# A scan and a delta-rule pass on one core: where the second begins, and where its helper work stands

## The chip, the core and the metric

The kernel runs on one core of a Trainium2 chip. TensorE (PE) multiplies, VectorE (DVE), ScalarE (ACT) and GpSimd (POOL) do elementwise work, and SyncE (SP) issues most DMAs. Each engine takes its instructions strictly in its own program order and waits on semaphores that others raise. The metric is the device time of one execution in microseconds (us), the median of three runs. All times below are in us.

## The reference

The reference is two transformer-like blocks over 1024 tokens of width 1024. The change lies in the first block's mixer, which has three branches that are concatenated:

- windowed attention with sinks (4 heads),
- a state-space scan (8 heads), with a state carried from chunk to chunk,
- a gated delta rule (4 heads of 64). For each chunk it solves a unit lower triangular system and then runs a recurrence over the chunks:

```
strict = tril((kbeta k^T) * decay, -1)
u, w   = solve(I + strict, [v*beta, kbeta*exp(g)])
v_new  = u - w state
o      = (q*exp(g)) state + (q k^T * decay) v_new
state  = state*exp(g_last) + (k*exp(g_last-g))^T v_new
```

The mixed output goes through `w_out`, and then a feed-forward and a second block of attention and gated mixing follow.

## The kernel before, in words

Tokens are cut into 8 chunks of 128. All engines walk one list, `schedule(units)`, of items `(kind, argument)`. Each engine's program is that list, filtered to the kinds that it has work for, so an item's place in the list sets its place in the queue of every engine that it touches. PE's products for such items go through four PSUM banks in rotation: a product needs its bank's earlier content read, four products before.

**The scan** (one iteration per chunk c, line 186 on) treats attention and state space together: `sa` makes the decay exponentials of a chunk (PE, then ACT L1256), `sg` multiplies them by C·B (DVE L1665), `as` scores and row maxima (PE L885, DVE L1618 to L1623, ACT exponentials L1231), `ap` transposes the attention weights (PE L893, copied by ACT L1237 and DVE L1629), `ao` applies them (PE L906, DVE L1635), `yo` and `yd` are the two parts of the output (DVE L1726, L1731), `st` updates the state `Sst` (PE L988, DVE L1734) and has POOL gate the output (L751 to L755). POOL also scales the inputs of a chunk (`xc`, L746, L748) as part of `sa`; its second scaling waits for ACT.

**The inverses.** The delta rule's triangular systems are inverted by blocks. The 32x32 diagonal blocks of all chunks and heads lie on the 128 partitions of one tile `AB` (they came there through DRAM), and DVE inverts them all together in 31 elimination steps, items `inv`, each a multiply (L1675) and a subtract (L1677) over up to 16x16 elements. Six steps stand at the end of each scan chunk from chunk 1 on, so the 31st, with a copy (L1679), stands in chunk 6. SP then stores both results to DRAM and loads them back as blocks with 16 DMAs into `qkv` (L688 to L695, semaphore `x_in`). In SP's program this stands behind the loads of `z` for the scan (L642), of which the one for chunk 7 waits until chunk 5 is gated.

**The delta pass** handles chunk c with these items: `gx` expands the 32-blocks into the block-diagonal 128x128 matrices `X` and `XT` (8 ACT instructions of L1287; POOL scales keys and values into `kbv`, L763 to L765), `ly` and `lx` (PE L958 and L970, read out by DVE L1695, L1702, L1704) merge blocks to size 64 (level 5) and 128 (level 6), `uw` applies the inverse (PE L994, L997, copied by ACT L1298), `r1` and `r2` are the recurrence (PE L1004 to L1012, DVE L1709 to L1717, ACT squares L1274). X, XT and Y have three buffers. The order is software-pipelined: iteration c runs the recurrence of chunk c, level 6 of chunk c+1, level 5 of chunk c+2, and at its end the expansion of chunk c+3.

**The norms.** `sn` 0 and `sn` 1 normalise the scan's output for chunks 0 to 3 and 4 to 7: a reciprocal square root in 12 short DVE instructions (L1412 to L1418), then 8 ACT instructions (L1270). `gn` is the like for the delta rule (DVE, then POOL). `mx` transposes everything for the product with `w_out`.

Of the kernel before, what the change touches and what calls it, by code (L numbers as in the profile page):

```python
# [25 lines left out]
NT = T // P  # L26
# [114 lines left out]
NORMED = (3, 6, 7)  # L141
# [7 lines left out]
def schedule(units):  # L149

    by = {u["kind"]: n for n, u in enumerate(units)}
    s, late, begun = [], [], set()

    def begin(kds, before, between):

        begun.update(kds)
        s.extend(before + [("half", (by[kd], 0)) for kd in kds] + between + [("half", (by[kd], 1)) for kd in kds])
# [26 lines left out]
    steps = iter(range(31))  # L184
    s += [("sa", 0), ("as", 0), ("sg", 0), ("sa", 1), ("yo", 0)]
    for c in range(NT):
        more = c + 1 < NT
        s += [("yd", c), ("ap", c), ("st", c)] + [("sg", c + 1), ("as", c + 1)] * more + [("ao", c)]
        s += [("yo", c + 1)] * more + [("sa", c + 2)] * (c + 2 < NT) + [("inv", n) for n in islice(steps, 6 * (c > 0))]
        s += [("sn", c // 4)] * (c % 4 == 3)  # L190
    assert next(steps, None) is None


    def at(kind, c, lv=None):
        return [(kind, c if lv is None else (c, lv))] if 0 <= c < NT else []
# [1652 lines left out]
```

How the kernel before makes its waits and increments, by code:

```python
        def gemm_product(eng, n):  # L494
            eng.wait_ge(gemm_done[n % 2], wide(n) // 2 + 1)
# [1 line left out]
        def gemm_consumed(eng, n):  # L498
            eng.wait_ge(gemm_read[n % 2], wide(n) // 2 + 1)
# [1 line left out]
        def scores_product(eng, h):  # L502
            w = scores_number(h)
            eng.wait_ge(gemm_done[w % 2], w // 2 + 1)
            return G[w % 2]
# [1 line left out]
        def scores_consumed(eng, h):  # L508
            w = scores_number(h)
            eng.wait_ge(gemm_read[w % 2], w // 2 + 1)
# [1 line left out]
        def side_product(eng, key):  # L513
            p = prod[key]
            eng.wait_ge(side_done[p % 4], p // 4 + 1)
            return S[p % 4]
# [1 line left out]
        def side_consumed(eng, key):  # L519
            p = prod[key]
            eng.wait_ge(side_read[p % 4], p // 4 + 1)
# [7 lines left out]
            def __call__(self, ins, name=None):  # L530
                s = N[name] if name else self.own
                self.count[name] = self.count.get(name, 0) + 1
                ins.then_inc(s, 1)
                self.eng.wait_ge(s, self.count[name])
# [1 line left out]
            def frees(self, ins, key):  # L536
                p = prod[key]
                ins.then_inc(side_read[p % 4], 1)
                self.eng.wait_ge(side_read[p % 4], p // 4 + 1)
# [1 line left out]
            def frees_gemm(self, ins, n):  # L542
                ins.then_inc(gemm_read[n % 2], 1)
                self.eng.wait_ge(gemm_read[n % 2], wide(n) // 2 + 1)
# [89 lines left out]
            def load_z(c):  # L635
                if c >= 2:
                    sp.wait_ge(N["gated"], c - 1)
                else:
```

## Time and profile before

| | us |
|---|---|
| runs | 2437.78, 2437.77, 2436.27 |
| median | 2437.77 |
| the profiled execution, its own time | 2435.77 |
| its span, first to last instruction | 2433.9 |
| mean granted TensorE clock, share of full | 0.965 |
| PE busy | 2224.6 (91%) |
| DVE, ACT, POOL busy | 954.6, 697.1, 621.2 |
| the scan, first to last chunk | 386 to 512 |
| the delta pass, first to last product | 523.8 to 615.5 |

A "busy" time adds up what an engine's instructions took; the chain of waits says which of them set the end. Positions are us from the start of the span. The granted clock is a share of 2.4 GHz; 0.50 is 1.2 GHz. "Idle before" in a timeline row is how long an engine stood in front of that instruction, and the name behind the arrow is whose end released it.

### The profile page before, as it was taken

To read this page: it belongs to the slowest core of one execution; us is meant where nothing else is said; L and a number is where in the kernel's file an instruction comes from. 1 tells how busy PE (TensorE), PEld (TensorE's weight loads), DVE (VectorE), ACT (ScalarE), POOL (GpSimd) and SP (SyncE) were. 2 spreads that over 40 slices of the span, in tenths; PEclk is the share of its full clock that TensorE was granted. 3 is DMA by queue.
4 is the path that set the end of the run, shared out by engine and by line. 5 is a ranking of instruction groups with operands and counts; after the bars stand their busy time and mean duration, and the time that the engine had idled before them with its cause. 6 is when DMAs were issued, how large, how long until landed. Compare 5 with 4: busy or idle time off the path is not lost.

```text
span 2433.9 us, 28528 instructions
## 1 busy us (share of the span) xinstructions
PE 2224.6 (91%) x11363; PEld 1878.0 (77%) x11363; DVE 954.6 (39%) x1429; ACT 697.1 (29%) x1478; POOL 621.2 (26%) x399
## 2 busy tenths in 40 slices
PE   6999988768987999999999996978999999999896
PEld 5888877667777888888888875767888888888775
DVE  4445316856315101211121125678995235111123
ACT  4332135444333111000000005327775122000134
POOL 2233322322221323323233331220000233233321
PEclk9999999779998999999999997999999999999998
DMA  4111310020310111111111110300001111111121
GB/s 147 44 44 44 93 33 24 18 70 1 104 44 27 45 51 52 44 53 44 52 52 44 52 44 27 114 27 10 1 1 31 44 45 43 52 48 48 52 95 69
DMA packets 179475, 117.51 MB, mean 48 GB/s; under 512 B 25252, under 2 KB 171408, under 8 KB 179216
## 3 DMA queue, kind: packets, MB, share of 16 engines
q1 hardware_dynamic: 165984, 91.77, 13.0%
q10 hardware_dynamic: 13360, 23.92, 2.8%
q8 instruction: 90, 1.47, 0.3%
q14 instruction: 41, 0.34, 0.0%
HBM read 102.57 MB, written 13.11 MB: 48 GB/s over the span
## 4 chain that ended last, share of the span: by engine, by line
PE 73%; DVE 18%; ACT 5%; issue 2%; SPq 1%; DMA 0%; ACTq 0%; DVEq 0%
PE gemm L811 21%; PE gemm L813 21%; PE gemm L812 21%; DVE PT L1426 3%; DVE a2m L1787 3%; PE side L842 2%; PE side L822 2%; PE side L970 1%; DVE x L1749 1%; ACT sqp L1112 1%; DVE rpd L1591 1%; PE side L1047 1%; DVE w_raw L1677 1%; PE side L958 1%; ACT Eg L1246 0%
## 5 line engine op out<-in xcount | busy, mean ns | idle before, releaser
L811 PE MATMUL gemm<-h_hi,w_hi 128*128 128x512 f32 x1968 | 773.8, 393 | 8.2 <-DVE h_lo L1819 8.2
L813 PE MATMUL gemm<-h_hi,w_lo 128*128 128x512 f32 x1968 | 768.3, 390 | 0.0
L812 PE MATMUL gemm<-h_lo,w_hi 128*128 128x512 f32 x1968 | 768.0, 390 | 0.0
L714 POOL TENSOR_SCALAR w_hi<-w_raw 128x1024 fp32r<-128x1024 f32 x153 | 170.3, 1113 | 1539.5 <-PE gemm L813 1524.3
L811 PEld LDWEIGHTS gemm<-h_hi,w_hi 128*128 128x128 f32 x1968 | 370.6, 188 | 86.1 <-issue 8.1
L813 PEld LDWEIGHTS gemm<-h_hi,w_lo 128*128 128x128 f32 x1968 | 370.3, 188 | 77.5
L812 PEld LDWEIGHTS gemm<-h_lo,w_hi 128*128 128x128 f32 x1968 | 370.8, 188 | 75.0
L716 POOL TENSOR_TENSOR w_lo<-w_raw,w_hi 128x1024 fp32r<-128x1024 f32 x153 | 374.4, 2447 | 12.8
L1450 DVE TENSOR_TENSOR ft<-sg,gemm 128x1024 f32<-128x1024 f32 x22 | 26.9, 1221 | 382.1 <-PE gemm L813 382.1
L811 PE MATMUL gemm<-f_hi,w_hi 128*128 128x512 f32 x352 | 138.9, 395 | 4.9 <-DVE f_lo L1452 4.9
L1160 ACT ACTIVATE f_hi<-ft 128x1024 fp32r<-128x1024 f32 x22 | 23.4, 1064 | 414.2 <-DVE ft L1450 414.2
L813 PE MATMUL gemm<-f_hi,w_lo 128*128 128x512 f32 x352 | 138.1, 392 | 0.0
L812 PE MATMUL gemm<-f_lo,w_hi 128*128 128x512 f32 x352 | 138.1, 392 | 0.0
L1456 DVE TENSOR_TENSOR accT<-accT,gemm 128x1024 f32<-128x1024 f32 x40 | 48.8, 1221 | 172.3 <-PE gemm L813 172.1
L1445 DVE SCALAR_TENSOR_TENSOR cacc<-cin,cols,cacc 128x1024 f32<-128x1024 f32 x42 | 67.4, 1606 | 89.3 <-ACT cacc L1132 88.3
L1059 PE MATMUL side<-PT,vp 128*128 128x256 f32 x512 | 92.4, 302 | 0.4 <-DVE PT L1426 0.4
L1426 DVE TENSOR_TENSOR PT<-side,PT 128x512 fp32r<-128x512 f32 x128 | 88.5, 691 | 10.0 <-ACT PT L1369 6.2
L1369 ACT ACTIVATE PT<-side 128x512 fp32r<-128x512 f32 x128 | 76.5, 598 | 44.2 <-PE side L1047 39.9
L1047 PE MATMUL side<-con,Pb 128*128 128x128 f32 x512 | 77.9, 276 | 9.5 <-DVE aoT L1803 9.5
L811 PEld LDWEIGHTS gemm<-f_hi,w_hi 128*128 128x128 f32 x352 | 66.8, 190 | 18.9 <-issue 5.3
L1470 DVE TENSOR_TENSOR yT<-sig,gemm 128x1024 f32<-128x1024 f32 x8 | 9.8, 1221 | 181.8 <-PE gemm L813 181.8
L1787 DVE TENSOR_REDUCE a2m<-gemm 128x1 f32<-128x1024 f32 x64 | 78.4, 1224 | 5.8 <-PE gemm L1038 3.6
(348 smaller groups left out, 2719.5 us busy)
## 6 DMA issues: line engine op xcount, KB each, us to landing
w_raw<-in_w_in SPq DMA_DIRECT2D x60, 512.0 KB, 3.8
w_raw<-in_ffn_w_gate SPq DMA_DIRECT2D x22, 512.0 KB, 3.8
w_raw<-in_ffn_w_up SPq DMA_DIRECT2D x22, 512.0 KB, 3.8
w_raw<-in_ffn_w_down SPq DMA_DIRECT2D x22, 512.0 KB, 3.5
w_raw<-in_w_out SPq DMA_DIRECT2D x16, 512.0 KB, 4.2
xin<-in_x SPq DMA_DIRECT2D x8, 512.0 KB, 6.7
x<-in_x ACTq DMA_DIRECT2D x1, 4096.0 KB, 15.4
x_spill<-x ACTq DMA_DIRECT2D x2, 2048.0 KB, 7.1
```

The source lines that it names most:

```text
L714: gp.tensor_scalar(whi[w % 2][:], raw[w % 4][:], 1.0, 0.0, ALU.mult, ALU.add).then_inc(pool_hi, 1)
L716: gp.tensor_tensor(wlo[w % 2][:], raw[w % 4][:], whi[w % 2][:], ALU.subtract).then_inc(w_split, 1)
L811: mm(o, hi[:, k, m], act[0][:, k, t], start=k == 0, stop=False)
L812: mm(o, hi[:, k, m], act[1][:, k, t], start=False, stop=False)
L813: last = mm(o, lo[:, k, m], act[0][:, k, t], start=False, stop=k == kt - 1)
L1047: last = tr(b[:, hslice(i)], Pb[(2 * m + i % 2) % 4][:, hslice(2 * q + i // 2)], ident)
L1059: last = mm(b[:, 0:256], vp[:, 2 * q + i, m % 4 // 2, :], PT[q][part][:, 256 * i:256 * i + 256], start=q == 0 and i == 0 and part == 0, st ...
L1369: step(af(PT[q][0][:], b[:], ACT.Copy), "hi_ready")
L1426: ins = v.tensor_tensor(dst, b, hi, ALU.subtract)
L1445: step(v.scalar_tensor_tensor(out=buf[:], in0=cin[:, i:i + T], scalar=cols[:, wcol:wcol + 1], in1=buf[:], op0=ALU.mult, op1=ALU.add), "con ...
L1456: step.frees_gemm(v.tensor_tensor(accT[:, j[1], :], accT[:, j[1], :], g[:], ALU.add), n)
L1787: step(v.reduce_max(mx, g[:], axis=AX))
```

## The change

Only the list in `schedule` changes. The elimination steps stand eight to a chunk from chunk 1 on, so that the last stands in chunk 4. The last scan chunk also takes in the first items of the delta pass (`gi`, three `gx`, the merges of chunk 0, level 5 of chunk 1, `uw` of chunk 0). In the delta pass `gx` stands at the start of an iteration instead of the end, and `sn` 1, which stood at the end of the scan, stands at the end of the pass's iteration 1. Line numbers of the changed kernel are 2 higher from there on.

```diff
@@ -185,20 +185,22 @@
     s += [("sa", 0), ("as", 0), ("sg", 0), ("sa", 1), ("yo", 0)]
     for c in range(NT):
         more = c + 1 < NT
-        s += [("yd", c), ("ap", c), ("st", c)] + [("sg", c + 1), ("as", c + 1)] * more + [("ao", c)]
-        s += [("yo", c + 1)] * more + [("sa", c + 2)] * (c + 2 < NT) + [("inv", n) for n in islice(steps, 6 * (c > 0))]
-        s += [("sn", c // 4)] * (c % 4 == 3)
+        if more:
+            s += [("yd", c), ("ap", c), ("st", c), ("sg", c + 1), ("as", c + 1), ("ao", c), ("yo", c + 1)]
+            s += [("sa", c + 2)] * (c + 2 < NT) + [("inv", n) for n in islice(steps, 8 * (c > 0))] + [("sn", 0)] * (c == 3)
+        else:
+            s += [("gi", 0), ("gx", 0), ("yd", c), ("ap", c), ("ly", (0, 5)), ("gx", 1), ("st", c), ("lx", (0, 5)), ("ao", c)]
+            s += [("ly", (0, 6)), ("ly", (1, 5)), ("lx", (0, 6)), ("lx", (1, 5)), ("uw", 0), ("gx", 2)]
     assert next(steps, None) is None
 
 
     def at(kind, c, lv=None):
         return [(kind, c if lv is None else (c, lv))] if 0 <= c < NT else []
 
-    s.append(("gi", 0))
-    for c in range(-3, NT):
-        s += at("ly", c + 1, 6) + at("r1", c) + at("ly", c + 2, 5) + at("lx", c + 1, 6) + at("r2", c)
-        s += at("lx", c + 2, 5) + at("uw", c + 1) + at("gx", c + 3)
-        s += [("gn", n) for n in range(len(NORMED) - 1) if NORMED[n] == c]
+    for c in range(NT):
+        s += at("gx", c + 3) + at("ly", c + 1, 6) + at("r1", c) + at("ly", c + 2, 5) + at("lx", c + 1, 6) + at("r2", c)
+        s += at("lx", c + 2, 5) + at("uw", c + 1)
+        s += [("gn", n) for n in range(len(NORMED) - 1) if NORMED[n] == c] + [("sn", 1)] * (c == 1)
     begin([("wo", 0), ("wo", 1)], [("mx", 0)], [("gn", len(NORMED) - 1), ("mx", 1), ("load", 0)])
     run([("wo", j) for j in range(8)], lambda kd: [(0, ("woT", kd[1]))])
     flush()
```

No instruction is added or taken away on any engine; the places move. Names are buffers, `x4` is four like instructions in a row.

**ACT, end of the scan, before.** From the row sums of the last scan chunk's scores (`asb`) to the second read-out of a solved block (`uw`); `X_148`, `X_149`, `X_150` are the three expansion buffers.
```order
L1231 ACTIVATE asb,asum<-asb,anm 128x256 x4
L1232 ACTIVATE ads<-ads 128x4
L1237 ACTIVATE apT<-side 128x512
L1264 ACTIVATE mixs_145,nss_s<-xs 128x256 x2
L1270 ACTIVATE xs<-xs,nrs_s 128x256 x8
L1287 ACTIVATE X_148<-qkv,con 128x4x32 x4
L1287 ACTIVATE XT_151<-qkv,con 128x4x32 x4
L1287 ACTIVATE X_149<-qkv,con 128x4x32 x4
L1287 ACTIVATE XT_152<-qkv,con 128x4x32 x4
L1298 ACTIVATE uw_157<-side 128x512
L1287 ACTIVATE X_150<-qkv,con 128x4x32 x4
L1287 ACTIVATE XT_153<-qkv,con 128x4x32 x4
```

The same stretch of ACT in the changed kernel:
```order
L1233 ACTIVATE asb,asum<-asb,anm 128x256 x4
L1234 ACTIVATE ads<-ads 128x4
L1289 ACTIVATE X_148<-qkv,con 128x4x32 x4
L1289 ACTIVATE XT_151<-qkv,con 128x4x32 x4
L1239 ACTIVATE apT<-side 128x512
L1289 ACTIVATE X_149<-qkv,con 128x4x32 x4
L1289 ACTIVATE XT_152<-qkv,con 128x4x32 x4
L1266 ACTIVATE mixs_145,nss_s<-xs 128x256 x2
L1300 ACTIVATE uw_157<-side 128x512
L1289 ACTIVATE X_150<-qkv,con 128x4x32 x4
L1289 ACTIVATE XT_153<-qkv,con 128x4x32 x4
L1289 ACTIVATE X_148<-qkv,con 128x4x32 x4
```

The expansions of chunks 0 and 1 moved ahead of the copy of `apT` and of the squares, and the eight instructions of L1270 left this stretch.

**ACT inside the delta pass, before.** From the squares of chunk 0's output (`gsq`) on; `uw_158` and `uw_157` are the copies that chunk 1's and chunk 2's recurrence need.
```order
L1274 ACTIVATE gsq,nss_g<-qkv 128x64 x4
L1298 ACTIVATE uw_158<-side 128x512
L1287 ACTIVATE X_148<-qkv,con 128x4x32 x4
L1287 ACTIVATE XT_151<-qkv,con 128x4x32 x4
L1274 ACTIVATE gsq,nss_g<-qkv 128x64 x4
L1298 ACTIVATE uw_157<-side 128x512
L1287 ACTIVATE X_149<-qkv,con 128x4x32 x4
L1287 ACTIVATE XT_152<-qkv,con 128x4x32 x4
L1274 ACTIVATE gsq,nss_g<-qkv 128x64 x4
```

The same stretch in the changed kernel:
```order
L1276 ACTIVATE gsq,nss_g<-qkv 128x64 x4
L1300 ACTIVATE uw_158<-side 128x512
L1289 ACTIVATE X_149<-qkv,con 128x4x32 x4
L1289 ACTIVATE XT_152<-qkv,con 128x4x32 x4
L1276 ACTIVATE gsq,nss_g<-qkv 128x64 x4
L1300 ACTIVATE uw_157<-side 128x512
L1272 ACTIVATE xs<-xs,nrs_s 128x256 x8
L1289 ACTIVATE X_150<-qkv,con 128x4x32 x4
L1289 ACTIVATE XT_153<-qkv,con 128x4x32 x4
L1276 ACTIVATE gsq,nss_g<-qkv 128x64 x4
L1300 ACTIVATE uw_158<-side 128x512
```

The expansion (`X`, `XT`) moved from behind the `uw` copy to ahead of the squares, and the eight instructions on `xs` now stand between the copy of `uw_157` for chunk 2 and the expansion behind it.

**PE, last scan chunk, before.** `E_139` is that chunk's decay matrix, `asb` the attention weights, `Bt` and `av` the state update and the attention output; `SQ_114` belongs to chunk 0 of the delta rule.
```order
L985 MATMUL side<-xc_141,E_139 128x64 x8
L893 MATMUL side<-con,asb 128x128 x8
L988 MATMUL side<-xc_141,Bt 128x256 x2
L906 MATMUL side<-av,apT 128x64 x8
L958 MATMUL side<-X_148,SQ_114 128x128 x4
L970 MATMUL side<-Y_154,XT_151 128x128 x4
L970 MATMUL side<-XT_151,Y_154 128x128 x4
L958 MATMUL side<-X_148,SQ_114 128x128 x4
L958 MATMUL side<-X_149,SQ_115 128x128 x4
```

The same stretch in the changed kernel:
```order
L987 MATMUL side<-xc_141,E_139 128x64 x8
L895 MATMUL side<-con,asb 128x128 x8
L960 MATMUL side<-X_148,SQ_114 128x128 x4
L990 MATMUL side<-xc_141,Bt 128x256 x2
L972 MATMUL side<-Y_154,XT_151 128x128 x4
L972 MATMUL side<-XT_151,Y_154 128x128 x4
L908 MATMUL side<-av,apT 128x64 x8
L960 MATMUL side<-X_148,SQ_114 128x128 x4
L960 MATMUL side<-X_149,SQ_115 128x128 x4
```

The first merge product (`X_148`, `SQ_114`) moved ahead of the state update, and two more ahead of the attention output.

## Rows read from the trace of the kernel before

**Rows 1.** Windows by stage: length, busy PE, PEld, DVE, ACT, POOL, clock, DMA, GB/s.
```profile
414.65:429.10 14.45, 12.22 (x77) 10.89 (x77) 13.08 (x32) 7.73 (x25) 6.88 (x6) 0.88 0.07 19
443.47:462.25 18.78, 11.48 (x69) 9.11 (x68) 17.38 (x41) 10.18 (x30) 7.05 (x7) 0.74 0.06 16
462.25:484.32 22.07, 17.52 (x85) 15.23 (x86) 14.97 (x29) 9.34 (x28) 5.70 (x6) 0.73 0.04 12
484.32:497.58 13.26, 12.02 (x79) 10.86 (x79) 12.27 (x29) 7.72 (x25) 3.48 (x5) 0.91 0.07 21
512.20:523.83 11.63, 0.00 (x1) 0.00 (x1) 2.64 (x14) 7.29 (x17) 0.62 (x1) 0.50 0.86 190
523.83:537.69 13.86, 12.17 (x81) 11.20 (x81) 5.37 (x8) 3.19 (x8) 0.00 (x0) 0.74 0.22 54
537.69:604.30 66.61, 53.16 (x459) 50.58 (x457) 39.86 (x79) 31.21 (x102) 16.38 (x26) 0.97 0.01 1
```
**Rows 2.** Windows of DVE alone, in which it has no wait: length, busy, clock, DMA, GB/s.
```profile
420.83:425.80 4.97, 4.17 (x15) 0.94 0.01 3
435.22:436.75 1.53, 1.40 (x4) 1.00 0.00 0
436.75:440.17 3.42, 3.15 (x8) 1.00 0.00 0
449.57:458.95 9.38, 8.54 (x24) 0.66 0.00 1
449.60:453.26 3.66, 3.39 (x9) 0.90 0.00 0
474.45:481.02 6.57, 6.13 (x12) 1.00 0.00 0
490.41:494.28 3.87, 3.42 (x14) 1.00 0.00 0
503.71:505.25 1.54, 1.44 (x4) 0.50 0.00 0
512.20:514.91 2.71, 2.30 (x12) 0.50 0.78 123
```
**Rows 3.** Timeline of DVE, then POOL, chunk 3: start, us, operation.
```profile
450.96 0.42 DVE L1677 TENSOR_TENSOR w_raw<-w_raw,w_raw 128x252 f32<-128x252 f32 x1
...
454.63 1.14 DVE L1677 TENSOR_TENSOR w_raw<-w_raw,w_raw 128x252 f32<-128x252 f32 x1
...
454.29 1.21 POOL L748 TENSOR_TENSOR xc<-xc,ed 128x512 f32<-128x512 f32 x1 [8.30 <-ACT ed L1258]
```
**Rows 4.** Timeline of SP's queue: the last spill load of the scan.
```profile
484.50 0.32 SPq L642 DMA_DIRECT2D zs<-z_spill  x1
```
**Rows 5.** Chain of waits, before the first expansion.
```profile
517.55 2.72 DMA qkv<-x_blocks
```
**Rows 6.** Timeline of ACT: end of scan, start of pass; idle before in brackets.
```profile
504.20 0.20 ACT L1232 ACTIVATE ads<-ads 128x4 f32<-128x4 f32 x1
...
514.97 4.29 ACT L1270 ACTIVATE xs<-xs,nrs_s 128x256 f32<-128x256 f32 x8 [5.14 <-DVE nrs_s L1418]
520.34 1.70 ACT L1287 ACTIVATE X<-qkv,con 128x128 f32<-128x128 f32 x4 [1.08 <-DMA qkv<-x_blocks]
...
537.87 0.60 ACT L1298 ACTIVATE uw<-side 128x512 f32<-128x512 f32 x1 [10.62 <-PE side L997]
538.49 1.70 ACT L1287 ACTIVATE X<-qkv,con 128x128 f32<-128x128 f32 x4
...
546.00 0.26 ACT L1274 ACTIVATE gsq<-qkv 128x64 f32<-128x64 f32 x1 [4.07 <-DVE qkv L1714]
```
**Rows 7.** Timeline of PE: state update and attention output of the last scan chunk.
```profile
506.22 1.92 PE L988 MATMUL side<-xc,Bt 128*128 128x256 f32 x4
507.92 3.52 PE L906 MATMUL side<-av,apT 128*128 128x64 f32 x16
```
**Rows 8.** Waits in 537.69 to 604.30: us in total, times, longest.
```profile
PE side L958 <- ACT XT L1287: 13.5, 6, 2.2
```

## The prediction, made before the changed kernel was run

> **What bounds the kernel now.** I read the page's chain of waits first. It lies on PE for 73% of the span, nearly all of it in the large products, which the change leaves alone. The 240 us that it touches lie at 386 to 622, where the chain passes between engines, so I cut that stretch into windows [rows 1].
>
> A scan chunk takes 13.26 us when little else is in it, and in the one window of that length DVE still holds six inverse steps. The next window to look at is 512.20 to 523.83: 11.63 us in which PE does nothing. The last scan product has ended and the first merge product waits for an expansion, which waits for the inverses to come back from DRAM: the last of 16 loads lands at 517.55 + 2.72 = 520.27 [rows 5], ACT expands from 520.34 [rows 6], and DVE had the inverses ready at 505.25 [rows 2]. So the return trip is 15.0 us. Then come 13.86 us of lead-in, partly at half clock, before iteration 0 of the pass [rows 1].
>
> In the pass PE stands in front of its level 5 product six times, 13.5 us in all, always for ACT's expansion [rows 8], which ACT can only start behind its `uw` copy [rows 6]. In that window PE is busy 53.2 of 66.6 us, DVE 39.9, ACT 31.2 [rows 1].
>
> **What the change costs in the scan.** Call the inverse stretch the time on DVE between the end of its update of `Sst` (L1727) and the start of `mixs` (L1731). In chunk 1 it is 4.97 us and the chunk 14.45; in chunk 5 it is 3.87 and the chunk 13.26 [rows 1, 2]. What exceeds about 3.8 us lengthens the chunk one for one; below that, ACT's exponentials are last anyway. Chunk 3 fits: 9.38 - 3.85 + 13.26 = 18.79, measured 18.78.
>
> With eight steps a chunk, the stretches become:
> - Chunk 1: 4.97 + steps 7 and 8, 1.53 = 6.50.
> - Chunk 2: steps 9 to 12, 3.42, and 13 to 16, 3.66 = 7.1.
> - Chunk 3: its present 9.38 loses steps 13 to 16 (3.66) and gains steps 19 to 24, which take 6.57 in chunk 4, of which 1.4 is the stall below = 10.9.
> - Chunk 4: steps 25 to 30, 3.87, and step 31 with the copy, 1.54 = 5.4.
> - Chunks 5 and 6: none, and that gains nothing, since they were hidden there.
>
> Now the stall. A DVE step of 252 elements takes 0.42 us, but 1.14 when it begins after POOL's `xc` has begun [rows 3], and two such losses of 0.72 are in the 9.38 of chunk 3 and in the 6.57 of chunk 4. POOL's two instructions begin 4.72 us after the stretch does (449.57 to 454.29). The stretches of chunks 1 and 2 end at about that point now, and will reach past it. I add 1.4 to each of the first two and to chunk 4: 7.9, 8.5, 10.9, 6.8, against 4.97, 5.0, 9.38, 6.57. The scan grows by 3.0 + 3.5 + 1.5 + 0.2 = 8.2 us. Without any new stall it would be 5.3 (chunks 3 and 4 keep theirs), and if all are dodged 2.5.
>
> The Trainium skill says under "SBUF — State Buffer", section "SBUF: two separate sides", that DVE and POOL share a port pair as an exclusive lock: a DVE operation with two inputs in SBUF and a POOL operation that reads SBUF exclude each other for a whole instruction. By that rule every step that meets `xc` waits it out, and the rule speaks against longer stretches. The 1.14 against 0.42 above agrees, and a sum that ignored the rule would come out 2.9 us lower.
>
> PE also idles longer while DVE works, and after such idle time it comes back at 1.2 GHz: chunk 3's window has a clock of 0.74, and in chunk 4, 22.07 us long, 16.0 would follow from its 6.57 us stretch. Of the other 6.0, 4.3 is `sn` 0 on ACT (eight instructions like those at 514.97 [rows 6]), which leaves 1.7 for the clock. I take 1.5 us more in total, bounds 0 and 12 (twice those 6.0). Scan: +9.7.
>
> **What is gained between scan and pass.** Times here are those of before; the scan's delay is already counted. The inverses are ready at the end of chunk 4. SP must first issue the spill load that waits for chunk 5's gating (484.50 [rows 4]), so the return trip runs from there to about 484.8 + 15.0 = 499.8. ACT wants it at 504.40, when the last attention row is done [rows 6]. The margin is 4.6 us, and a longer scan shifts both alike. SP has nothing else queued between the two.
>
> The two halves of an expansion, X and XT, take 1.7 us each, 3.5 with the gap [rows 6], so PE's first merge product starts at 508.0 instead of 523.83: 15.8 earlier. From there to iteration 0 took 13.86. Into that now fall the state update, 1.92, and the attention output, 3.52 [rows 7], at half clock. The first lies where PE waited for DVE's read-out of Y (PE was idle 1.7 of the 13.86 [rows 1]), the second does not. PE has no long idle time before it, so some of this stretch may run at 2.4 GHz; I take the addition as 3.1 us, 1.92 + 3.52 less 1.7 and less 0.6 for this. Gain 12.7. The bounds: all at full clock 13.7; all at half clock, as the first half of the lead-in did, about 5.5.
>
> Queued behind the inserted work: ACT's copy of `apT` waits 3.5 us for the expansion, and `ao` waits for that copy. ao is then read at about 518, and only `zg` and weight loads on SP wait for it, needed 100 us later. POOL makes `kbv` of chunks 0 and 1 ahead of the gating, about 4 us, which nobody needs before `mx`. `uw` of chunk 0 is copied before the third expansion, as it was, so iteration 0 keeps its wait of 2.24.
>
> **What is gained in the pass.** From iteration 1 on the expansion stands one iteration ahead, so five of six waits go: 5 x 2.24 = 11.2. What is late next is PE itself: 66.6 / 6 = 11.1 us per iteration less 2.24 is 8.9, and PE is busy 53.2 / 6 = 8.9; ACT needs 31.2 / 6 = 5.2 and DVE 6.6 [rows 1].
>
> Two things lose their cover. `sn` 1 ran at 512 to 519, while everyone waited for the loads. Now its 2.71 us on DVE [rows 2] and 4.29 on ACT [rows 6] stand at the end of iteration 1. Behind them on ACT come the expansion 3.5, the squares about 1.5 and the `uw` copy 0.6: 12.6 us from the last `uw` copy to the end of the next, where PE wants the recurrence about 8.8 after it. Cost 3.8 us. And `gn` 0, 12 like instructions on DVE after iteration 3, was hidden by PE's 2.24 wait; without it about 0.9 of its 2.5 shows. Bounds: 2.0 for both if ACT's idle time absorbs more, 7.0 (2.71 + 4.29) if nothing overlaps. Pass: 11.2 - 3.8 - 0.9 = 6.5.
>
> **The sum.** 12.7 + 6.5 - 9.7 = 9.5 us less. The profiled execution took 2435.77 (span 2433.9 and 1.9 around it), which is 2.0 below the median of 2437.77. From the one, 2426.3; from the other, 2428.3. I predict 2428 for the median. Everything behind 622 shifts as a block: weights arrive and are split on their own queues, well ahead.
>
> **Rivals.**
> 1. *No stall, and a warm lead-in.* DVE's longer stretch slips between POOL's instructions, or the clock returns early. For: chunk 2's present stretch just misses `xc`. Against: POOL starts 4.72 after the stretch begins, whatever DVE does. 12.7 + 6.5 - 5.3 = 13.9, and 2424; with the lead-in at its best 2423.
> 2. *The pass does not speed up.* The expansion is early, but another wait takes its place, for instance the banks or the read-outs on DVE, busy 40 us of the 67. Against: DVE has over 2 us of room in each iteration of 8.9. The pass then gains nothing and still pays 4.7: 12.7 - 4.7 - 9.7 = -1.7, that is 2439, no change.
> 3. *PE's clock, the slower side.* The place is chunks 2 to 4 and the lead-in. If PE's idle gap behind each longer DVE stretch brings 1.2 GHz for most of the next chunk, as in the 22.07 us chunk, scores and decay products come late, DVE waits for them, and the gap grows again. Price: 6.0 in each of two more chunks, and the lead-in at its worst, 5.5. 5.5 + 6.5 - 8.2 - 12 = -8.2: 2446. It decides from about 12 us of extra scan time over the 8.2 with a cold lead-in; half of it gives no change. For it: 0.74 and 0.73 in rows 1. Against: chunk 1 ran at 0.88 and fits the formula without any clock term.
> 4. *The inverses come late.* If the return trip takes over 4.6 us longer beside the scan, ACT stands at the expansion with `apT` behind it, and each us more costs one. With 20 us in place of 15: hardly 1; with 25: 2434.
>
> The Trainium skill, "TensorE: Matmul & The Clock Gate", section "HAM oscillation — how this bites in real kernels", describes rival 3 as a rule: waits inside a loop re-throttle PE, and each round starts cold. Followed to the letter it gives the time of rival 3. The clock of 1.00 in the DVE windows of chunks 2 and 4 [rows 2] disagrees so far, the 0.66 of chunk 3 agrees.
>
> **Chances.** The forecast 58%, rival 1 18%, rival 2 8%, rival 3 8%, rival 4 8%. What the kernel's measurement can tell from no change is about 0.2%, 4.9 us, so faster ends at 2432.9. Forecast and rival 1 are on that side but for a few in a hundred, as is half of rival 4: 78%. Rival 2, the rest of rival 4, half of rival 3: 16%. Slower 6%. The range, 2419 to 2436, holds the first two with their bounds and most of rival 4.
>
> **What would show it.** In the new profile: PE's idle time in front of the first merge product about 1.5 us; the SP loads done before ACT's last attention exponential; waits of PE L960 on ACT's XT once, not six times; iterations of 8.6 to 8.9 us but for those behind iterations 1 and 3; DVE steps of 1.1 us in chunks 1 and 2; chunk lengths near 17.4, 17.9, 20.3 and 22 to 24. The forecast is wrong if the loads end behind 504 + 9.7, if chunks 5 and 6 got shorter than 13.26, or if the pass's six iterations take over 63 us (66.6 - 6.5 = 60.1 expected).

## The result, and the profile after

| | us |
|---|---|
| changed kernel, 4 runs | 2419.55 median (2418.59 to 2419.96) |
| kernel before, 4 runs beside it | 2437.78 median (2436.27 to 2442.52) |
| ratio | 0.9921, 95% interval 0.9904 to 0.9939 |
| profiled execution after: own time, span, mean clock | 2419.96, 2418.1, 0.969 |

The kernel got 18.2 us faster (0.8%), where 9.8 was forecast (2428 against 2419.55): the sign was right, and the forecast was about half of what came. From span to span the two profiled executions differ by 15.8 us (2433.9 to 2418.1). The rest of the 18.2 is that the profiled execution of before was 2.0 us quicker than its median and that of the changed kernel 0.4 slower.

First the same windows as in [rows 1], in the profile of the changed kernel: chunks 1 to 5, from the last chunk's scores to the first merge product, the lead-in, iterations 0 to 5, and the rest up to the first product with `w_out`. Columns as there.

```profile
413.77:431.22 17.45, 12.01 (x77) 10.48 (x77) 15.94 (x36) 7.73 (x25) 8.04 (x7) 0.86 0.05 16
431.22:449.99 18.77, 13.52 (x79) 11.62 (x79) 16.90 (x34) 7.72 (x25) 5.72 (x6) 0.86 0.05 14
449.99:470.20 20.21, 12.20 (x75) 10.07 (x74) 18.67 (x45) 10.18 (x30) 5.71 (x6) 0.75 0.05 15
470.20:492.66 22.46, 17.60 (x85) 15.17 (x86) 15.26 (x33) 9.34 (x28) 5.73 (x6) 0.73 0.04 12
492.66:505.82 13.16, 11.93 (x79) 10.78 (x78) 8.84 (x17) 7.73 (x25) 3.38 (x5) 0.92 0.60 152
505.82:516.16 10.34, 6.10 (x47) 5.54 (x46) 7.80 (x17) 6.86 (x22) 5.10 (x7) 0.95 0.23 36
516.16:530.62 14.46, 14.46 (x100) 13.71 (x100) 6.64 (x11) 4.81 (x13) 4.60 (x5) 0.80 0.32 93
530.62:589.77 59.15, 52.59 (x458) 50.43 (x456) 41.87 (x91) 35.31 (x110) 16.42 (x26) 0.97 0.06 15
589.77:607.45 17.68, 12.78 (x107) 11.23 (x105) 12.89 (x32) 7.98 (x25) 4.02 (x6) 1.00 0.00 1
```

Set against before, stretch by stretch:

| stretch | before | after | less by |
|---|---|---|---|
| start of chunk 1 (untouched code) | 414.65 | 413.77 | 0.9 |
| chunks 1 to 5 | 14.45, 14.37, 18.78, 22.07, 13.26 | 17.45, 18.77, 20.21, 22.46, 13.16 | -9.1 |
| chunk 6's start to iteration 0 | 40.11 | 24.80 | 15.3 |
| iterations 0 to 5 | 66.61 | 59.15 | 7.5 |
| iteration 6 to `w_out` | 17.68 | 17.68 | 0.0 |
| from there on (untouched code) | 1811.92 | 1810.65 | 1.3 |

**The scan.** These are the windows of DVE's inverse stretches of chunks 1 to 4, which answer to [rows 2].

```profile
419.93:427.92 7.99, 7.03 (x19) 0.91 0.01 2
438.04:446.69 8.65, 8.07 (x18) 1.00 0.00 0
456.08:466.91 10.83, 9.84 (x29) 0.71 0.00 0
482.39:489.36 6.97, 6.42 (x16) 1.00 0.00 0
```

Forecast were 7.9, 8.5, 10.9 and 6.8. The stall that was to come into chunk 1 is there. In DVE's and then POOL's timeline of that chunk, two steps of over 1 us, each beside one POOL instruction, stand in front of one of 0.36, as in [rows 3]:

```profile
424.92 1.06 DVE L1677 TENSOR_TENSOR w_raw<-AB,w_raw 128x175 f32<-128x175 f32 x1
426.02 1.08 DVE L1679 TENSOR_TENSOR w_raw<-w_raw,w_raw 128x175 f32<-128x175 f32 x1
427.14 0.36 DVE L1677 TENSOR_TENSOR w_raw<-AB,w_raw 128x192 f32<-128x192 f32 x1
...
424.66 1.12 POOL L750 TENSOR_TENSOR xc<-xc,ed 128x512 f32<-128x512 f32 x1 [7.25 <-ACT ed L1260]
425.87 1.04 POOL L753 TENSOR_TENSOR xs<-xs,dskip 128x512 f32<-128x512 f32 x1
```

**The return trip and the start.** SP's timeline, then ACT's, at the end of the scan:

```profile
492.84 0.32 SPq L644 DMA_DIRECT2D zs<-z_spill  x1
498.98 8.63 SPq L697 DMA_DIRECT2D qkv<-x_blocks  x16
...
512.44 0.20 ACT L1234 ACTIVATE ads<-ads 128x4 f32<-128x4 f32 x1
512.67 1.71 ACT L1289 ACTIVATE X<-qkv,con 128x128 f32<-128x128 f32 x4
```

The trip to DRAM begins right behind the spill load that waits for chunk 5 (492.84), the last of the 16 loads is issued by 498.98 + 8.63 = 507.6, and ACT goes from its last attention row (512.44) into the expansion without a gap [rows 4 to 6 for before]. PE's idle time in front of the first merge product is 2.38 us instead of 12.39 (about 1.5 was forecast). Its timeline from there:

```profile
516.16 2.07 PE L960 MATMUL side<-X,SQ 128*128 128x128 f32 x8 [2.38 <-ACT XT L1289]
518.03 1.91 PE L990 MATMUL side<-xc,Bt 128*128 128x256 f32 x4
519.74 1.91 PE L972 MATMUL side<-Y,XT 128*128 128x128 f32 x8
521.44 1.34 PE L972 MATMUL side<-XT,Y 128*128 128x128 f32 x8
522.62 1.90 PE L908 MATMUL side<-av,apT 128*128 128x64 f32 x16
```

The attention output took 1.90 here and not the 3.52 of [rows 7]: the clock came back to 2.4 GHz in the second merge (the granted clock is 0.50 up to 522.0, which is 5.9 us behind the start of the first merge product, and 0.97 from there to 522.62). In before it was 0.50 up to 531.0, 7.2 us behind that product. From the first merge product to iteration 0 it is 14.46 us, where 13.86 + 3.1 = 17.0 were forecast.

**The pass.** PE's waits in iterations 0 to 5, against the six of [rows 8]:

```profile
PE side L1006 <- issue: 2.5, 1, 2.5
PE side L960 <- ACT XT L1289: 2.2, 1, 2.2
PE side L972 <- DVE Y L1697: 1.8, 2, 0.9
```

The iterations take 12.46, 8.32, 9.44, 11.09, 9.52 and 8.32 us (before 10.83, 10.83, 12.45, 10.83, 10.84, 10.83). The 12.46 and the 12.45 are the same thing: 1.6 us of half clock behind a wait, which falls into one iteration of each kernel. The "issue" wait of 2.5 us stands in front of the recurrence of the 11.09 us iteration, and ACT's timeline shows what is late there:

```profile
551.58 0.60 ACT L1300 ACTIVATE uw<-side 128x512 f32<-128x512 f32 x1 [1.21 <-PE side L999]
554.52 4.29 ACT L1272 ACTIVATE xs<-xs,nrs_s 128x256 f32<-128x256 f32 x8 [2.34 <-DVE nrs_s L1420]
...
563.84 0.60 ACT L1300 ACTIVATE uw<-side 128x512 f32<-128x512 f32 x1
```

12.3 us from one `uw` copy to the next, because `sn` 1 stands between them (12.6 had been worked out).

### The profile page after: what moved, and what is told of

Read it like the earlier page. It is cut to its first block, busy times and chain, and to the rows that moved or that the text cites. A ratio compares the mean times of both kernels' runs of the same rounds, so it can differ in the third digit from the quotient of the medians.

```text
span 2418.1 us, 28528 instructions
## 1 busy us (share of the span) xinstructions
PE 2218.9 (92%) x11363; PEld 1873.2 (77%) x11363; DVE 957.3 (40%) x1429; ACT 697.7 (29%) x1478; POOL 621.7 (26%) x399
## 4 chain that ended last, share of the span: by engine, by line
PE 74%; DVE 18%; ACT 5%; issue 2%; SPq 0%; DMA 0%; ACTq 0%; DVEq 0%
PE gemm L813 21%; PE gemm L815 21%; PE gemm L814 21%; DVE PT L1428 3%; DVE a2m L1789 3%; PE side L844 2%; PE side L824 2%; DVE x L1751 1%; PE side L972 1%; ACT sqp L1114 1%; DVE rpd L1593 1%; DVE w_raw L1677 1%; DVE w_raw L1679 1%; PE side L1049 1%; PE side L960 1%
## 5 line engine op out<-in xcount | busy, mean ns | idle before, releaser
L1452 DVE TENSOR_TENSOR ft<-sg,gemm 128x1024 f32<-128x1024 f32 x22 | 26.9, 1221 | 382.0 <-PE gemm L815 382.0
L1428 DVE TENSOR_TENSOR PT<-side,PT 128x512 fp32r<-128x512 f32 x128 | 88.5, 691 | 10.1 <-ACT PT L1371 6.2
```

The costliest lines, as they stand in the source:

```text
L1428: ins = v.tensor_tensor(dst, b, hi, ALU.subtract)
```

## The experiments

Each ratio is to runs of the kernel before that were taken beside it: its median was 2436.95 for the first four kernels below, 2438.47 for the next four, 2436.73 for e8 to e10, and 2439.61 for e11. Where a text compares with the changed kernel, its 2419.6 is meant.

### The changed kernel once more (a0)

No edit; a yardstick for what repeats.

> The changed kernel once more, as the yardstick of this group. Its profiled span was 15.8 us below before's, its median 18.2. Theory (the profiled windows hold the whole effect): 14.5 us between 386 and the first w_out product, so a median 14 to 17 below before, and 18.2 was partly scatter. Rival (a real gain outside that stretch): 18 or more again.

2419.72 (2418.69 to 2420.82), ratio 0.9926 [0.9912, 0.9940]. Span 2418.9, chunks 17.45, 18.77, 20.24, 22.50, 13.17, iterations 12.46, 8.32, 9.45, 11.09, 9.52, 8.32, and 1810.7 from `w_out` on. The median is 17.2 below that of before, which is just above the theory's 14 to 17 and below the rival's 18. In these two profiled executions even the patches of half clock fall in the same places. That this holds for every execution of a program isn't shown: the kernel before was profiled once, and its executions range from 2433.5 to 2443.7, at mean clocks from 0.963 to 0.968.

### Eight steps alone (e1)

```diff
 kernel before:
-... [("inv", n) for n in islice(steps, 6 * (c > 0))]
+... [("inv", n) for n in islice(steps, 8 * (c > 0))]
```

> Before with eight elimination steps per chunk and nothing else. Theory: the scan grows by 9.1 us as in the changed kernel (chunks 1 to 4 about 17.5, 18.8, 20.2, 22.5), the inverses are back before the scan ends, but ACT still has sn 1 in front of the first expansion, so the first merge product stands at 519.3 + 0.3 + 3.5 + 9.1 = 532 instead of 523.8: slower than before by 8. Rival (the return trip from DRAM was the bound, so having it early pays by itself): the 11.6 us gap shrinks to under 3 and the kernel is faster than before.

2443.68 (2442.60 to 2447.79), ratio 1.0028 [1.0017, 1.0038]: 6.7 us slower than before, where 8 was expected. Chunks 17.45, 18.78, 20.22, 22.44, 13.17, those of the changed kernel to 0.03 us. The first merge product stands at 528.52 (before 523.83), since the end of the scan and `sn` 1 behind it (on ACT until 525.00), not the return trip, now decide. From the start of chunk 1 to iteration 0 it is 5.8 us more than before. Iterations 0 to 4 are as before, but iteration 5 took 12.46 instead of 10.83 and the stretch from iteration 6 to `w_out` 18.7 instead of 17.7, in code without an edit. So the steps' own cost is 5.8 us by the trace. It is real, and by itself it buys nothing.

### Expansion one iteration ahead alone (e2)

```diff
 kernel before:
-        s += at("ly", c + 1, 6) + at("r1", c) + at("ly", c + 2, 5) + ...
+        s += at("gx", c + 3) * (c >= 0) + at("ly", c + 1, 6) + at("r1", c) + at("ly", c + 2, 5) + ...
...
-        s += at("lx", c + 2, 5) + at("uw", c + 1) + at("gx", c + 3)
+        s += at("lx", c + 2, 5) + at("uw", c + 1) + at("gx", c + 3) * (c < 0)
```

> Before with gx of the pass at the start of an iteration and nothing else. Theory: five of six waits on ACT's XT go, each worth 2.5 us (10.83 to 8.32 per iteration), gn 0 shows 1.2 us: 12.5 - 1.2 = 11.3 faster. My prediction priced a wait at 2.24: 11.2 - 0.9 = 10.3. Rival (the early start of the pass is what pays): under 5.

2422.42 (2416.47 to 2425.33), ratio 0.9937 [0.9923, 0.9951]: 14.5 us faster than before, the greatest part of the change, where 11.3 was expected; its six runs scatter by 9 us. Iterations 10.83, 8.33, 8.32, 8.32, 9.53, 8.32 = 53.65, 13.0 less than 66.61. That is 5 x 2.51 = 12.5 for the waits, 1.6 for the clock patch that is gone, and 1.2 lost where `gn` 0 now shows (9.53). `sn` 1 still stood in the gap of the return trip and cost nothing.

### The early start with six steps a chunk (e4)

```diff
 changed kernel:
-... [("inv", n) for n in islice(steps, 8 * (c > 0))]
+... [("inv", n) for n in islice(steps, 6 * (c > 0))]
```

> The changed kernel with six elimination steps per chunk, so that the last stands in chunk 6. Theory: the scan is 9.1 us shorter, but the inverses are ready only at 505 and land at 520.3 (positions of before), ACT stands at the first expansion with the copy of apT behind it, the merge product starts at 523.8, and with state update and attention output behind it iteration 0 starts 14.5 later at 538.3, against 531.5 in the changed kernel: 7 us slower than the changed kernel, 8 to 9 faster than before. Rival (the scan's growth costs more than the early return is worth): faster than the changed kernel.

2428.69 (2425.31 to 2428.90), ratio 0.9961 [0.9948, 0.9974]: 9.0 slower than the changed kernel, where 7 was expected. The chunks are those of before, but the first merge starts at 523.55. So eight steps, which lose 6.7 alone, gain 9.0 here (by the trace from chunk 1 to iteration 0: 5.8 lost, 5.6 gained): only both together bring the start forward. And this kernel is 6.3 slower than e2, which has none of the early start. Its iterations 0 to 5 take 60.7 us, 7.0 more than in e2: 3.9 is `sn` 1, which has lost its cover and gets nothing for it, and 3.1 are patches of half clock (iterations of 12.35 and 12.72).

### The second norm behind the pass (e3)

```diff
 changed kernel:
-        s += [... if NORMED[n] == c] + [("sn", 1)] * (c == 1)
-    begin(..., [("mx", 0)], [("gn", len(NORMED) - 1), ("mx", 1), ("load", 0)])
+        s += [... if NORMED[n] == c]
+    begin(..., [("mx", 0)], [("sn", 1), ("gn", len(NORMED) - 1), ("mx", 1), ("load", 0)])
```

> The changed kernel with sn 1 moved out of the pass to behind the first half of mx, where ACT is idle for 10 us and DVE for 7. Theory: the 1.1 us that PE waits for DVE's read-out of Y in iteration 2 and the 2.8 us before the recurrence of chunk 3 both go: 3.9 us faster than the changed kernel, iterations 2 and 3 of the pass 8.32 each. Rival (sn 1 is hidden there by slack): no change. Second rival: it now delays the second half of mx, and up to 2 us come back there.

2419.06 (2418.18 to 2421.42), ratio 0.9923 [0.9911, 0.9935]: 0.7 faster by the times, too little to tell from nothing. In the trace the pass is what was expected, iterations 12.47, 8.32, 8.32, 8.32, 9.53, 8.33 = 55.29, 3.9 less than 59.15, and the second half of `mx` comes no later. So `sn` 1 did cost 3.9. Chunks 3 to 5 were 2.1 us shorter, too. But the stretch from iteration 6 to `w_out` took 19.0 here instead of 17.7, at a clock of 0.82 where it was 1.00, and what is behind `w_out` 1812.9 instead of 1810.7; with that most of the gain is gone again. The 19.0 isn't the new place of `sn` 1, for e2 has 19.0 as well, without that edit. The last section shows one of the places behind `w_out`.

### POOL's multiply behind its wait (e5)

```diff
 changed kernel, POOL, item st:
-   step(gp.tensor_tensor(h64(xs[:, c, :]), h64(xs[:, c, :]), widen(dskip[:], 64), ALU.mult))
    side_consumed(pool, (("yd", c), 0))
+   step(gp.tensor_tensor(h64(xs[:, c, :]), h64(xs[:, c, :]), widen(dskip[:], 64), ALU.mult))
```

> The changed kernel with POOL's multiplication by dskip behind its wait for yd instead of ahead of it, so that only one POOL instruction instead of two falls into each inverse stretch of DVE. Theory (DVE steps wait for a POOL instruction that has begun): one DVE instruction of 1.1 us less per chunk, stretches of chunks 1 to 4 shorter by 0.7 each, 2.9 us faster than the changed kernel. Rival (the slow DVE steps are something else, for instance the steps' own shapes): no change, and the slow steps stay in number.

2416.65 (2415.33 to 2417.38), ratio 0.9911 [0.9898, 0.9923]: 3.1 faster than the changed kernel, where 2.9 was expected. The same steps of chunk 1 (DVE, then POOL) show one long step instead of two:

```profile
425.64 1.06 DVE L1677 TENSOR_TENSOR w_raw<-AB,w_raw 128x175 f32<-128x175 f32 x1
426.73 0.34 DVE L1679 TENSOR_TENSOR w_raw<-w_raw,w_raw 128x175 f32<-128x175 f32 x1
...
425.38 1.13 POOL L750 TENSOR_TENSOR xc<-xc,ed 128x512 f32<-128x512 f32 x1 [7.25 <-ACT ed L1260]
428.73 1.04 POOL L754 TENSOR_TENSOR xs<-xs,dskip 128x512 f32<-128x512 f32 x1 [2.23 <-DVE mixs L1733]
```

Chunks 1 and 2 are 0.73 us shorter each (16.72, 18.04), the price of one collision. DVE's stretches of chunks 3 and 4 are shorter, too (10.1 and 5.4 instead of 10.8 and 7.0; in chunk 4 two collisions went). Chunk 3 stayed at 20.25 all the same, because its stretch began 0.7 later in the chunk. Chunks 4 and 5 are 19.00 + 14.14 instead of 22.46 + 13.16: 2.5 less, of which 1.5 is the shorter stretch and the rest goes with the clock (0.85 instead of 0.73 in chunk 4). That the total fits the expected 2.9 is luck: the lead-in and iteration 0 were another 2.9 shorter by the clock, and the code behind the pass took 3.5 longer.

### State update and attention output ahead of the pass's items (e6)

```diff
 changed kernel:
-            s += [("gi", 0), ("gx", 0), ("yd", c), ("ap", c), ("ly", (0, 5)), ("gx", 1), ("st", c), ("lx", (0, 5)), ("ao", c)]
+            s += [("gi", 0), ("yd", c), ("ap", c), ("st", c), ("ao", c), ("gx", 0), ("ly", (0, 5)), ("gx", 1), ("lx", (0, 5))]
```

> The changed kernel with the last scan chunk's own items (yd, ap, st, ao) ahead of the first expansion and merge. Theory (the interleaving fills PE's waits of the lead-in): ACT's expansion starts after the copy of apT at about 514.4, ends at 518, PE runs st and ao in its shadow; the first merge product stands 2 us later than 516.2, the lead-in is about 2.5 us shorter: within 1 us of the changed kernel. My prediction's pricing (2.4 to 3.8 us for st and ao in the lead-in) would make it 1 to 2 us faster. Rival (keeping PE busy early brings 2.4 GHz back early, which this order loses): 3 us or more slower.

2426.89 (2425.05 to 2428.32), ratio 0.9953 [0.9941, 0.9965]: 7.3 slower, where the theory had under 1 and the rival 3 or more. The first merge product comes 14.65 us behind the start of the last window of the scan (DVE's second product with `E`) instead of 10.34. ACT, which takes its items in order, copied `apT` at 515.05, then stood at the squares until POOL had gated (517.51), and began the expansion only at 518.59. The lead-in took 15.62 instead of 14.46, with 16 products of L960 at half clock (3.79 instead of 2.00). Together that is 5.5 us. The rest isn't the edit's: in the profiled execution chunk 1 began 3.8 later than in the changed kernel, in code that is the same.

### Both norms late (e7)

```diff
 e3, and in it:
-            s += [...] + [("inv", n) ...] + [("sn", 0)] * (c == 3)
+            s += [...] + [("inv", n) ...]
...
-        s += [... if NORMED[n] == c]
+        s += [... if NORMED[n] == c] + [("sn", 0)] * (c == 4)
```

> As e3 (sn 1 behind the first half of mx), and sn 0 also out of the scan, to the end of iteration 4 of the pass. Theory: chunk 3's stretch loses 2.4 us of DVE, chunk 4 loses 4.3 us of ACT and part of its slow clock (22.5 to about 17 to 18); in the pass it costs about 1.2 on DVE and under 1 on ACT. Sum: 2.4 + 4.3 + 1 - 2 = about 6 faster than e3, about 10 faster than the changed kernel. Rival (sn 0 is as dear in the pass as it was in the scan): 3.9 lost again in the pass, about 3 faster than e3.

2416.99 (2416.32 to 2417.42), ratio 0.9913 [0.9898, 0.9927]: 2.1 faster than e3, where the theory had about 6 and the rival 3. Chunks 3 and 4 fall to 18.33 and 15.84 (from 20.21 and 22.46), and iteration 5 of the pass grows from 8.3 to 13.33. So the norm cost 5.0 us in its new place. In DVE's and PE's timeline there, every second of the norm's twelve short instructions takes 0.5 to 0.6 us instead of 0.17, PE waits 3.11 for Y, and comes back at half clock:

```profile
571.38 0.60 DVE L1414 TENSOR_SCALAR nv<-nss_s 128x8 f32<-128x8 f32 x1
572.01 0.17 DVE L1415 TENSOR_SCALAR nrs_s<-nv 128x8 int32<-128x8 int32 x1
572.22 0.58 DVE L1416 TENSOR_SCALAR nv<-nv 128x8 f32<-128x8 f32 x1
...
576.81 1.78 PE L972 MATMUL side<-XT,Y 128*128 128x128 f32 x8 [3.11 <-DVE Y L1697]
```

### State update and attention output behind the first `uw` (e8)

```diff
 changed kernel:
-            s += [..., ("ly", (0, 5)), ("gx", 1), ("st", c), ("lx", (0, 5)), ("ao", c)]
-            s += [("ly", (0, 6)), ("ly", (1, 5)), ("lx", (0, 6)), ("lx", (1, 5)), ("uw", 0), ("gx", 2)]
+            s += [..., ("ly", (0, 5)), ("gx", 1), ("lx", (0, 5))]
+            s += [("ly", (0, 6)), ("ly", (1, 5)), ("lx", (0, 6)), ("lx", (1, 5)), ("uw", 0), ("st", c), ("ao", c), ("gx", 2)]
```

> The changed kernel, with the last chunk's state update and attention output behind the first uw products instead of between the merges. It measures by itself the term that I priced at 3.1 us. Measure: from the start of the first merge product to the start of the first uw product on PE, 12.34 us before the change (523.83 to 536.17), 12.94 in the changed kernel (516.16 to 529.10). Theory (the two products filled gaps of PE of 0.85 and 0.84 us and kept it active, so that its clock came back earlier; their net price was 0.6): the distance comes out at 12.0 to 12.6, and the whole kernel within 2 us of the changed one (2419.7), since the 2 us that they take in their new place fall on the way to iteration 0's wait of 2.25. Rival (the price as I worked it out, 3.1 us): the distance falls to about 9.8 and the kernel gets 1 to 3 us faster.

2423.28 (2421.64 to 2424.66), ratio 0.9941 [0.9929, 0.9954]. This is the test of the term that I had mis-sized. PE's timeline, the two products now gone from it:

```profile
516.91 2.08 PE L960 MATMUL side<-X,SQ 128*128 128x128 f32 x8 [2.38 <-ACT XT L1289]
519.84 2.07 PE L972 MATMUL side<-Y,XT 128*128 128x128 f32 x8 [0.85 <-DVE Y L1697]
...
524.06 2.05 PE L960 MATMUL side<-X,SQ 128*128 128x128 f32 x16 [0.84 <-DVE X L1704]
...
529.21 1.00 PE L996 MATMUL side<-kbv,XT 128*128 128x64 f32 x8
```

The gaps of 0.85 and 0.84 are back, and a third of 0.31, and from the first merge to the `uw` product it takes 529.21 - 516.91 = 12.30 us, against 12.94 with both products in it. They cost 0.64 us in their place, not 3.1. But the half of my theory that says that they bring the clock back earlier finds no support: without them the clock came back just as early, 5.8 us behind the first merge product (0.50 up to 522.5, 1.00 from 522.7). Behind `uw` the two products cost 2.7 (530.73 to 533.43), of which iteration 0 gave back 1.6 of its wait (0.68 instead of 2.25). The squares of the last chunk also moved on ACT, in front of the expansion. The kernel is 3.6 slower, where I had expected it within 2, yet lead-in and iteration 0 together are 1.2 us shorter (25.7 for 26.9), with a patch of half clock of 1.6 gone from iteration 0; one of 1.4 came in iteration 3. The loss lies behind the pass, 0.7 up to `w_out` and 2.2 from there on, where nothing was edited.

### The first norm in a gap of ACT (e9), and three edits together (e10)

```diff
 changed kernel (e9):
-            s += [("yd", c), ("ap", c), ("st", c), ...]
-            s += [...] + [("inv", n) ...] + [("sn", 0)] * (c == 3)
+            s += [("yd", c), ("ap", c)] + [("sn", 0)] * (c == 5) + [("st", c), ...]
+            s += [...] + [("inv", n) ...]
```

e10 has this edit and those of e3 and e5.

> The changed kernel, with the first norm (sn 0) in scan chunk 5 between the attention transpose and the state update, instead of behind chunk 3's inverse steps. There ACT stands idle for 5.0 us behind its copy of the transposed weights, and DVE for 2.4 us in front of the update of Sst. Theory: chunks 3 and 4 together lose the 2.7 us of DVE and the 4.3 us of ACT (42.7 to about 35.7, less or more with the clock), chunk 5 grows by under 1.5, and the kernel comes to about 2413.5 (2411 to 2416). Rival (idle time of ACT and DVE in a chunk of 13.2 us is not free, because ACT's row sets the chunk): chunk 5 grows by 4 to 7 us, the total stays at 2419 to 2420.

> The changed kernel with three edits at once: POOL's multiply by the skip weights behind its wait for the output product (3.1 us less by itself), the second norm behind the first half of the mixed transposes (3.9 less in the pass by its trace, 0.7 by its time), and the first norm in chunk 5's gap (6 less by the theory). Theory (the gains lie in different stretches and add): 2407 (2404 to 2410). Rival (clock of PE takes back what is gained, as it did where the second norm was moved): 2411 to 2415.

e9: 2417.99 (2416.20 to 2419.98), ratio 0.9921 [0.9907, 0.9934], where 2413.5 was expected. Chunks 3 and 4 took 17.87 + 20.67 = 38.5 instead of 42.7, chunk 5 stayed at 13.16: its rival, that chunk 5 grows, is out, but 2.8 us less than expected were gained in chunks 3 and 4. e10: 2413.41 (2412.89 to 2413.82), ratio 0.9902 [0.9886, 0.9917], chunks 16.72, 18.04, 17.83, 20.11, 13.15: inside the rival's range. But the rival's reason, the clock, was not the whole of it, for chunk 4 ran at 0.92. I had misread the order of DVE. An item of chunk 5 in front of its state update stands, on DVE, directly behind chunk 4's inverse steps, where DVE has no idle time. In e10's timeline of DVE (the first and the last of the twelve, and one between):

```profile
480.21 0.17 DVE L1414 TENSOR_SCALAR nv<-nss_s 128x8 f32<-128x8 f32 x1
...
480.63 1.12 DVE L1416 TENSOR_SCALAR nv<-nv 128x8 f32<-128x8 f32 x1
...
485.06 0.17 DVE L1420 SCALAR_TENSOR_TENSOR nrs_s<-nt__70,nrs_s 128x8 f32<-128x8 f32 x1
```

5.05 us from the first to the next instruction behind them. The same twelve take 2.42 in chunk 3 of the changed kernel (464.49 to 466.91), where none of them meets POOL; the 2.71 of [rows 2] hold one that did, at 512.40, of 0.46 us.

### The same, with the norm one chunk later (e11)

```diff
 e10:
-            s += [("yd", c), ("ap", c)] + [("sn", 0)] * (c == 5) + [("st", c), ...]
+            s += [("yd", c), ("ap", c)] + [("sn", 0)] * (c == 6) + [("st", c), ...]
```

> The kernel with the three edits together, with the first norm (sn 0) one scan chunk later: between the attention transpose and the state update of chunk 6 instead of chunk 5. In the kernel with three edits its 12 short DVE instructions stood right behind the last inverse steps, where DVE is never idle: they took 480.21 to 485.26, 5.05 us instead of 2.7, since POOL ran its gating beside them, and so chunk 4 took 20.11. One chunk later DVE waits 1.5 and 2.4 us in front of the two instructions around them. Theory: chunk 4 falls to about 15.1, chunk 5 grows from 13.15 to between 13.4 and 15.7 (the part of 2.7 to 5.1 us that its 2.4 us of idle time doesn't cover), and the kernel comes to 2410 (2408.5 to 2411.5) instead of 2413.4. Rival (the price of chunk 4 is that of PE's clock, which the idle time behind DVE's work takes down): chunk 4 stays above 18, and the kernel within 1.5 us of 2413.4.

2405.06 (2404.14 to 2410.64), ratio 0.9867 [0.9851, 0.9884]: 8.4 us faster than e10 and the fastest of all, where 2410 (2408.5 to 2411.5) was expected. Its windows of chunks 4 and 5, the lead-in and iterations 0 to 5:

```profile
464.93:479.74 14.81, 13.27 (x81) 11.56 (x81) 13.71 (x33) 7.73 (x25) 6.15 (x5) 0.88 0.06 18
479.74:497.13 17.39, 12.27 (x85) 10.83 (x84) 14.22 (x29) 9.04 (x28) 7.00 (x7) 0.97 0.59 137
507.48:519.38 11.90, 11.90 (x100) 11.07 (x100) 6.64 (x11) 4.80 (x13) 5.08 (x6) 1.00 0.38 113
519.38:573.02 53.64, 50.46 (x458) 48.65 (x456) 39.85 (x79) 31.23 (x102) 16.38 (x26) 1.00 0.07 16
```

Chunk 4 fell by 5.3 to 14.81, as the theory said. Chunk 5 grew by 4.2 instead of 0.3 to 2.6: the norm's DVE part met POOL again (5.79 us) and its idle time hid little. By the norm alone 1.1 us was won. The rest came unasked, in code that stands as in e10: chunks 2 and 3 were 1.4 us shorter (17.40 and 17.08), the lead-in ran at a clock of 1.00 and took 11.90 instead of 14.26, iterations 0 to 5 lost their patch of 1.6, the stretch from iteration 6 to `w_out` took 17.7 instead of 19.1, and what is behind it 1.0 less. These 7.8 us of the 9.2 between the spans are in no theory of mine, so the size of this gain must not be put down to the edit.

## Why the prediction was half right

**The scan, +9.7: right.** It grew by 9.1. The stretches were forecast to 0.2 us, and the stall in chunks 1 and 2 came by the rule that [rows 3] had shown. e1 shows the cost by itself, in the same chunks. Of the 1.5 for PE's clock 0.6 came, nearly all in chunk 2 (18.77, where the formula gives 18.1).

**The return trip: right.** It ran behind the spill load and was over before ACT wanted it. The first merge came 15.9 earlier, set against the scan's delay; forecast 15.8. Rival 4 is out.

**The lead-in: the step that failed.** I wrote: "I take the addition as 3.1 us, 1.92 + 3.52 less 1.7 and less 0.6 for this." It was 0.6 (14.46 against 13.86), and e8 measures the same quantity as 0.64, with the clock coming back at the same place to 0.1 us. The start gained 15.3 instead of 12.7. The rows show where the two terms of the addition went. From start to start the two products take 1.71 + 1.74 = 3.45 (518.03 to 519.74, 522.62 to 524.36), priced at 5.44. The other products from the first merge to the `uw` product take 12.94 - 3.45 = 9.49, where all of it took 12.34 before: 2.85 less, of which 1.69 are the gaps of 0.85 and 0.84 that are filled. I had taken off 2.3.

So the greater part is the price. I used the half-clock 3.52 of [rows 7] for the attention output. Nor does that number belong to its old place: in e1 and e2, where the product stands in the same place of PE's order, it took 1.97. The 3.52 was a patch of half clock that before happened to have there. At full clock I had allowed 2.1 at the least; the filled gaps and the neighbours' clock made it less.

How much less is partly luck. In the other kernels with this order the lead-in took 14.5 (a0), 14.4 (e3), 13.6 (e4), 13.2 (e5), 13.4 (e7), 13.3 (e9), 14.3 (e10) and 11.9 (e11), and it goes with the clock, which came back 5.9, 5.8, 4.0, 3.2, 3.7, 3.4 and 5.4 us behind the start of the first merge product and in e11 had not fallen at all. So against before's one lead-in the addition lies between 0.6 and -2.0, always below my least.

**The pass, 6.5: nearly right.** It was 7.5. Each wait that goes is worth 10.83 - 8.32 = 2.51, not 2.24, five times. A likely reason is that without the wait the next product is also pipelined into the one before it: L960 now starts 0.45 behind L1008, whose own time is 0.61, and takes 1.06 instead of 1.16, together 0.26. The two norms cost 3.9 (e3 shows it) and 1.2; forecast were 3.8 and 0.9. Rival 2 is out by the iterations of 8.32, rival 3 by chunk lengths and by the lead-in.

**The sum.** 15.3 + 7.5 - 9.1 = 13.7, in place of 9.5; the lead-in is 2.6 of the 4.2 between them. Another 2.2 us of the 15.8 between the spans are in code that the change does not touch (0.9 ahead of it, 1.3 behind it). Between the medians 17.2 (a0) or 18.2 us are measured; the 1.4 to 2.4 us above 15.8 no trace shows, because before was profiled once. So only half of the miss of 8.4 us lies in the terms of my sum. The range (2419 to 2436) just holds the result. Rival 1 (2423: no new stall, and a warm lead-in) came nearer in the number, but half of it was wrong, for chunks 1 and 2 have the stall.

**Additivity.** Eight steps -6.7, expansion ahead +14.5, together +7.8, against 17.2 for the whole. The remaining 9.4, from which the 3.9 for `sn` 1 are already taken, belong to the early start. In the trace, from the start of chunk 1 to the end of iteration 5, the numbers are -7.5 (1.6 of it a patch of half clock in e1's iteration 5), +14.0 and +13.7, which leaves 5.6 to 7.2 for it. The early start exists only when the steps are early (e4), and 5.5 us of it only when its items are woven between the scan's (e6).

## What to carry to other kernels

Price a moved instruction by the gaps of the place where it goes, and at both clocks: a duration read at half clock need not come back even in the same place (3.52 in before, 1.97 in e1). A step that costs on its own (e1) can be what another step needs (e4), so try such parts together as well as apart. And when a helper such as a norm loses its cover, look for the idle time of every engine that it uses, in that engine's own order: `sn` 0 had a free gap on ACT and none on DVE.

## What was not expected of the hardware

**PE's patches of half clock differ from program to program, in code that has no edit.** Chunks 4 and 5 took 22.1 to 22.5 + 13.2 us in before, the changed kernel, a0, e1 and e4, 18.6 to 19.6 + 14.3 in e2, e3 and e6, and 21.6 + 14.3 in e8, though e2 has the same items there as before, and e3, e6 and e8 those of the changed kernel. The start of chunk 1, ahead of every edit, lies between 413.3 and 417.6, and what is behind `w_out` took from 1810.7 to 1813.0. What picks one or the other isn't shown. One place where it parts is the norm products behind 19.3 us of idle PE. PE's timeline of the changed kernel, and then of e10:

```profile
726.75 9.07 PE L844 MATMUL side<-diag,x 128*128 128x128 f32 x64 [19.29 <-DVE diag L1501]
```

```profile
718.15 10.12 PE L844 MATMUL side<-diag,x 128*128 128x128 f32 x64 [19.27 <-DVE diag L1501]
```

The same 64 products after the same idle time differ by 1 us, by when the clock came back to 2.4 GHz: it is 0.50 in the first 1.85 us of both, then 0.59 in the next two us of the changed kernel and still 0.50 in those of e10, and 0.81 and 0.72 in the whole. In before they took 9.66. So one edit's effect in the total is uncertain by 2 to 3 us, and by 4 when the start of chunk 1 moves as in e6, even when its runs agree to 1 us; the stretch of the trace where the edit lies tells more than the total.

**Short DVE instructions wait for POOL too.** A 128x8 instruction of 0.17 us took up to 1.12 beside POOL's, and it ended 0.03 us after POOL's did (e7: POOL L774 ran 572.03 to 572.77, DVE L1416 ended at 572.80). Each POOL instruction that ran beside the norm held one of the twelve: six in e7, three in e10, four in e11. The Trainium skill, "SBUF — State Buffer", section "SBUF: two separate sides", calls the pair of ports an exclusive lock for a whole instruction; that agrees with these rows. Twelve tiny instructions (2.4 us when none meets POOL) so took 4.7 (e7), 5.1 (e10) or 5.8 (e11), while the large steps of the scan lost 0.7 each. It goes the other way, too. The copy of `AB` (L1681) took 1.76 in the changed kernel, where POOL's multiply had begun first. In e5 the copy began 0.41 us ahead of POOL's `xc` and took 1.07, and POOL's 1.04 became 1.57.
